# Delta-rule triangular solve: full 128 by 128 tiles against packed 64 by 64 blocks

## The reference, cut to what matters

```python
decay = jnp.exp(jnp.where(incl, gcum[..., :, None] - gcum[..., None, :], -jnp.inf))
kb = kc * bc[..., None]
a_mat = jnp.where(strict, jnp.einsum('nbhid,nbhjd->nbhij', kb, kc) * decay, 0.0) \
    + jnp.eye(c, dtype=jnp.float32)
rhs = jnp.concatenate([vc * bc[..., None], kb * jnp.exp(gcum)[..., None]], axis=-1)
sol = lax.linalg.triangular_solve(a_mat, rhs, left_side=True, lower=True, unit_diagonal=True)
u_val, k_cum = sol[..., :dv], sol[..., dv:]
qk = jnp.where(incl, jnp.einsum('nbhid,nbhjd->nbhij', qc, kc) * decay, 0.0)
```

## Time and profile before

| quantity | value |
|---|---|
| median of 3 runs | 1184.05 us (1181.15 to 1190.07) |
| the profiled execution, its own time | 1182.57 us |
| its span in the trace | 1180.8 us |
| PE busy | 1133.2 us (96%) |
| PE weight loads busy | 1029.1 us (87%) |
| DVE busy | 768.0 us (65%) |
| ACT busy | 553.0 us (47%) |
| the chain that ended last | PE 80%, DVE 12%, ACT 4%, issue 3%, DMA 1% |

### The profile page before, as it was taken

The page is one execution under the profiler, slowest core; times in us unless marked ns, Lnnn a source line. Parts: engine busy times, 40 slices in busy tenths (PEclk is TensorE's granted clock), DMA queues, the critical chain, the costliest instruction groups (busy, mean ns, idle before and its releaser), DMA issues.

```text
span 1180.8 us, 17834 instructions
## 1 busy us (share of the span) xinstructions
PE 1133.2 (96%) x7630; PEld 1029.1 (87%) x7630; DVE 768.0 (65%) x914; ACT 553.0 (47%) x639; POOL 45.2 (4%) x108
## 2 busy tenths in 40 slices
PE   7989998999999999999998899999999999999996
PEld 6888887898899899998788789999888998999995
DVE  4585767664477898887577565455556866555544
ACT  5466554332444444434564454444445565444443
POOL 8000000000000000000002200000000000000000
PEclk9999999999999999999999999999999999999999
DMA  7765864265354555555453355556543435566551
GB/s 248 201 165 78 130 142 115 56 124 87 112 193 154 188 185 196 183 179 178 147 189 123 127 180 179 182 194 193 179 143 107 142 110 178 181 192 195 182 178 54
DMA packets 128448, 185.08 MB, mean 157 GB/s; under 512 B 6868, under 2 KB 104161, under 8 KB 128370
## 3 DMA queue, kind: packets, MB, share of 16 engines
q1 hardware_dynamic: 123136, 182.46, 52.1%
q10 hardware_dynamic: 4690, 1.36, 0.5%
q0 software_dynamic: 544, 0.13, 0.1%
HBM read 182.89 MB, written 1.05 MB: 156 GB/s over the span
## 4 chain that ended last, share of the span: by engine, by line
PE 80%; DVE 12%; ACT 4%; issue 3%; DMA 1%; ACTq 0%; SPq 0%; DVEq 0%
PE ps L1916 13%; PE ps L1917 13%; PE ps L1918 13%; PE ps L1933 10%; PE ps L1934 10%; PE ps L1935 10%; DVE low L1278 4%; ACT whi L902 1%; PE ps L2250 1%; PE ps L1949 1%; PE ps L2120 1%; PE ps L2126 1%; PE ps L2129 1%; DMA raw<-in_w_in 1%; PE ps L1902 1%
## 5 line engine op out<-in xcount | busy, mean ns | idle before, releaser
L902 ACT ACTIVATE whi<-raw 128x2048 fp32r<-128x2048 f32 x172 | 328.0, 1912 | 346.2 <-PE ps L1918 169.8
L1278 DVE TENSOR_TENSOR low<-raw,whi 128x2048 fp32r<-128x2048 f32 x172 | 394.2, 2295 | 51.8 <-ACT whi L902 48.8
L1916 PE MATMUL ps<-hhi,whi 128*128 128x256 f32 x1424 | 410.3, 288 | 5.1 <-DVE low L1278 3.2
L1917 PE MATMUL ps<-hlo,whi 128*128 128x256 f32 x1424 | 405.7, 285 | 0.0
L1918 PE MATMUL ps<-hhi,low 128*128 128x256 f32 x1424 | 405.5, 285 | 0.0
L1916 PEld LDWEIGHTS ps<-hhi,whi 128*128 128x128 f32 x1424 | 275.6, 194 | 11.4 <-issue 4.7
L1917 PEld LDWEIGHTS ps<-hlo,whi 128*128 128x128 f32 x1424 | 275.8, 194 | 1.7 <-issue 0.2
L1918 PEld LDWEIGHTS ps<-hhi,low 128*128 128x128 f32 x1424 | 275.7, 194 | 0.0
L1933 PE MATMUL ps<-whi,ahi 128*128 128x512 f32 x416 | 163.9, 394 | 5.6 <-issue 1.8
L1934 PE MATMUL ps<-low,ahi 128*128 128x512 f32 x416 | 162.4, 390 | 0.0
L1935 PE MATMUL ps<-whi,alo 128*128 128x512 f32 x416 | 162.0, 390 | 0.0
(11 more groups left out here) (381 smaller groups left out, 1189.9 us busy)
## 6 DMA issues: line engine op xcount, KB each, us to landing
raw<-in_ffn_w SPq DMA_DIRECT2D x64, 1024.0 KB, 5.3
raw<-in_w_in SPq DMA_DIRECT2D x32, 1024.0 KB, 10.4
raw<-in_w_up SPq DMA_DIRECT2D x22, 1024.0 KB, 4.9
raw<-in_gla_w_in SPq DMA_DIRECT2D x12, 1024.0 KB, 5.2
raw<-in_w_down SPq DMA_DIRECT2D x11, 1024.0 KB, 4.8
raw<-in_ab_w_in SPq DMA_DIRECT2D x8, 1024.0 KB, 5.2
raw<-in_w_branch SPq DMA_DIRECT2D x6, 1024.0 KB, 5.8
raw<-in_w_o SPq DMA_DIRECT2D x4, 1024.0 KB, 4.8
```

The source lines that it names most:

```text
L902: act.activation(whi[:, u % SPLIT, :], raw[:, u % RAW, :], ACT.Copy).then_inc(sem("hi_done"), 1)
L1278: dve.tensor_tensor(wlo[:, u % RAW, :], raw[:, u % RAW, :], whi[:, u % SPLIT, :].bitcast(F32), ALU.subtract).then_inc(sem("lo_done"), 1)
L1916: pe.matmul(out, wh, hi[:, k0 + k, :], start=k == 0, stop=False)
L1917: pe.matmul(out, wh, lo[:, k0 + k, :], start=False, stop=False)
```

## The change

The chunk matrices are kept packed: partitions 0 to 63 hold the 64 by 64 matrices of the tile's first chunk, partitions 64 to 127 those of the second, heads side by side, so an array is 128 partitions by 256 columns. `chunks` are the two slices of 64 partitions. A product over four heads is issued as eight source matmuls (two chunks per head), each with rows 0 to 63 and columns 0 to 63 of the array, or rows 64 to 127 and columns 64 to 127, in turn. GpSimd makes packed copies of three constants, and `dn_pre(0)` on DVE waits for them. The key-key products use all 128 rows and one half of the columns; the second product of `dn_sol` uses one half of the rows and all columns and writes two banks. The order of the two z products and of the two updates is exchanged, and the last level leaves out X. `dn_x0` becomes a matmul with the packed identity in place of a transpose. The table of steps is the same.

```diff
+        def packed(one, half):
+            return by(one[:, half * DH * CH:(half + 1) * DH * CH], DH)
...
+        levp = own_[3][:, 0:6 * CH].rearrange("p (l j) -> p l j", l=6)
+        trip, idp = own_[3][:, 6 * CH:7 * CH], own_[3][:, 7 * CH:8 * CH]
+        chunks = [slice(CH * b, CH * b + CH) for b in range(P // CH)]
...
+            for c_ in chunks:
+                then(pool.tensor_copy(trip[c_, :], tri[c_, c_]))
+                then(pool.tensor_copy(idp[c_, :], ident[c_, c_]))
+                then(pool.tensor_copy(levp[c_, :, :], lev[c_, :, c_]))
...
             def dn_y(t, l):
                 act.wait_ge(sem("dn_BX"), 2 * (l - 1) + t + 1)
-                act.activation(Y[t], by(ps[:, 7 - t, :], DH), ACT.Copy).then_inc(sem("dn_Y"), 1)
+                act.activation(Y[t], packed(ps[:, 7 - t, :], 0), ACT.Copy).then_inc(sem("dn_Y"), 1)
...
             def dn_decay(t):
                 dve.wait_ge(sem("dn_eg"), t + 1)
-                link(dve.tensor_tensor(DT[t], by(ps[:, grow_bank[t], :], DH),
-                                       wide(gcol[:, t, :].unsqueeze(2), [DH, P]), ALU.subtract))
+                for c_ in chunks:
+                    ins = dve.tensor_tensor(DT[t][c_], by(ps[c_, grow_bank[t], :], DH)[:, :, c_],
+                                            gcol[c_, t, :].unsqueeze(2).to_broadcast([CH, DH, CH]), ALU.subtract)
+                link(ins)
...
             def dn_z(t, l):
                 n_ = 2 * (l - 1) + t + 1
-                dve.wait_ge(sem("dn_XBX"), 2 * n_)
-                own(dve.tensor_tensor(XT[t], XT[t], by(ps[:, 2 * t, :], DH), ALU.subtract), "dn_X2", 2 * n_ - 1)
-                own(dve.tensor_tensor(X[t], X[t], by(ps[:, 2 * t + 1, :], DH), ALU.subtract), "dn_X2", 2 * n_)
+                last = l == LEVELS - 1
+                if not last:
+                    dve.wait_ge(sem("dn_XBX"), 2 * n_ - 1)
+                    own(dve.tensor_tensor(X[t], X[t], packed(ps[:, 2 * t + 1, :], 0), ALU.subtract), "dn_X2", 2 * n_ - 1)
+                done = 4 * (l - 1) + t + 1 if last else 2 * n_
+                dve.wait_ge(sem("dn_XBX"), done)
+                own(dve.tensor_tensor(XT[t], XT[t], packed(ps[:, 2 * t, :], 0), ALU.subtract), "dn_X2", done)
...
             def dn_decay(t):
                 pe.wait_ge(sem("dn_gb"), 2 * t + 2)
-                pe.matmul(by(ps[:, beta_bank[t], :], DH), ones[:, :], XT[t], start=True, stop=True)
+                for c_ in chunks:
+                    pe.matmul(packed(ps[c_, beta_bank[t], :], 0), ones[c_, 0:CH], XT[t][c_], start=True, stop=True)
...
             def dn_kk(t):
                 for j in range(2):
                     for h in range(DH):
+                        for c_ in chunks:
+                            cols_ = slice(t * P + c_.start, t * P + c_.stop)
+                            ins = pe.matmul(ps[c_, kk_banks[t][j], h * CH:(h + 1) * CH], dnT[:, DH + h, cols_],
+                                            dnT[:, (DH if j == 0 else 0) + h, cols_], start=True, stop=True)
...
             def dn_z(t, l):
+                if l < LEVELS - 1:
+                    for h in range(DH):
+                        for c_ in chunks:
+                            ins = pe.matmul(ps[c_, 2 * t + 1, h * CH:(h + 1) * CH], XT[t][c_, h, :], Y[t][c_, h, :],
+                                            start=True, stop=True)
+                    ins.then_inc(sem("dn_XBX"), 1)
+                for h in range(DH):
+                    for c_ in chunks:
+                        ins = pe.matmul(ps[c_, 2 * t, h * CH:(h + 1) * CH], Y[t][c_, h, :], XT[t][c_, h, :],
+                                        start=True, stop=True)
                 ins.then_inc(sem("dn_XBX"), 1)
...
             def dn_sol(t):
-                pe.wait_ge(sem("dn_X2"), 2 * (8 + t + 1))
+                pe.wait_ge(sem("dn_X2"), 4 * (LEVELS - 2) + t + 1)
                 if t:
-                    pe.wait_ge(sem("dn_u"), t)
                     pe.wait_ge(sem("dn_kcT"), t)
                 for h in range(DH):
-                    ins = pe.matmul(ps[:, 6, h * P:(h + 1) * P], XT[t][:, h, :], vb[:, t, h, :], start=True, stop=True)
+                    for c_ in chunks:
+                        ins = pe.matmul(ps[c_, 2 * t + 1, h * P:(h + 1) * P], XT[t][c_, h, :], vb[c_, t, h, :],
+                                        start=True, stop=True)
                 for h in range(DH):
-                    ins = pe.matmul(ps[:, 7, h * P:(h + 1) * P], rhsk[:, t, h, :], XT[t][:, h, :], start=True, stop=True)
+                    for b, c_ in enumerate(chunks):
+                        ins = pe.matmul(ps[:, 6 + b, h * CH:(h + 1) * CH], rhsk[c_, t, h, :], XT[t][c_, h, :],
+                                        start=True, stop=True)
```

More of the change, by code:

```diff
@@ L16 @@
 SPLIT = 3
+LEVELS = 6
 LEAD = 2
@@ L662, in build @@
         flat = [cy[:, i, :, :].rearrange("p a t -> p (a t)") for i in range(2)]
-        DT = [by(one, DH) for one in (flat[1], own_[3])]
-        X, XT, LT, Bl, Y = [[by(one, DH), by(two, DH)] for one, two in
-                            zip(own_[0:3] + flat, tops + [own_[3]])]
+        def packed(one, half):
+            return by(one[:, half * DH * CH:(half + 1) * DH * CH], DH)
+        X, XT, LT, Bl = [[packed(a_, k), packed(b_, k)] for a_, b_, k in
+                         ((own_[0], tops[0], 0), (own_[1], tops[1], 0), (own_[1], tops[1], 1), (flat[0], tops[2], 0))]
+        Y = DT = [packed(flat[1], 0), packed(tops[2], 1)]
+        grows = [by(own_[0], DH), by(tops[0], DH)]
+        dnout = by(own_[2], DH)
+        levp = own_[3][:, 0:6 * CH].rearrange("p (l j) -> p l j", l=6)
+        trip, idp = own_[3][:, 6 * CH:7 * CH], own_[3][:, 7 * CH:8 * CH]
+        chunks = [slice(CH * b, CH * b + CH) for b in range(P // CH)]
         S = by(xs[:, 1, 0:512], DH)
@@ L1580, in dn_y @@
             def dn_y(t, l):
[L1581 removed]
+                dve.tensor_tensor(Bl[t], LT[t], wide(levp[:, l, :].unsqueeze(1), [DH, CH]), ALU.mult)\
                    .then_inc(sem("dn_B"), 1)
@@ L1629, in dn_out @@
                     dve.wait_ge(sem("dn_hi"), t)
-                own(dve.scalar_tensor_tensor(out=XT[0], in0=by(ps[:, 6, :], DH), scalar=col("dn_gain", 0),
+                own(dve.scalar_tensor_tensor(out=dnout, in0=by(ps[:, 6, :], DH), scalar=col("dn_gain", 0),
                                              in1=zT[:, :, t * P:(t + 1) * P], op0=ALU.mult, op1=ALU.mult),
@@ L2089, in dn_decay @@
                     pe.wait_ge(sem("dn_tok"), 6)
-                pe.matmul(by(ps[:, beta_bank[t], :], DH), ones[:, :], XT[t], start=True, stop=True)
-                pe.matmul(by(ps[:, grow_bank[t], :], DH), ones[:, :], X[t], start=True, stop=True)\
+                for c_ in chunks:
+                    pe.matmul(packed(ps[c_, beta_bank[t], :], 0), ones[c_, 0:CH], XT[t][c_], start=True, stop=True)
+                pe.matmul(by(ps[:, grow_bank[t], :], DH), ones[:, :], grows[t], start=True, stop=True)\
                   .then_inc(sem("dn_grow"), 1)
@@ L2125, in dn_z @@
                 for h in range(DH):
-                    ins = pe.matmul(ps[:, 2 * t, h * P:(h + 1) * P], Y[t][:, h, :], XT[t][:, h, :], start=True, stop=True)
-                ins.then_inc(sem("dn_XBX"), 1)
-                for h in range(DH):
-                    ins = pe.matmul(ps[:, 2 * t + 1, h * P:(h + 1) * P], XT[t][:, h, :], Y[t][:, h, :], start=True, stop=True)
+                    for c_ in chunks:
+                        ins = pe.matmul(ps[c_, 2 * t, h * CH:(h + 1) * CH], Y[t][c_, h, :], XT[t][c_, h, :],
+                                        start=True, stop=True)
@@ L2164, in dn_state @@
                         pe.matmul(out, dnT[:, h, c * CH:(c + 1) * CH], S[:, h, :], start=True, stop=False)
-                    ins = pe.matmul(out, qkT[own_, t, h, own_], vb[own_, t, h, :], start=c == 0, stop=True)
+                    ins = pe.matmul(out, qkT[own_, t, h, 0:CH], vb[own_, t, h, :], start=c == 0, stop=True)
                 ins.then_inc(sem("dn_o"), 1)
```

54 lines of the change are left out of this document (30 added, 24 removed).

## The result

Changed kernel: 1173.66 us median (1172.41 to 1175.25, 4 runs) against 1184.05 (1181.15 to 1190.07, 4 runs, one more than in the table ahead of the prediction); ratio 0.9914, 95% interval 0.9889 to 0.9939. The predicted 1167 was 6.7 too low. The range of 1163 to 1181 held the time, its likeliest part of 1163 to 1171 did not. The gain is 10.4 us, 0.86%; I had given 0.69 to a gain of over 1%. Run again beside another set of runs of before it came to 0.9904 (0.9874 to 0.9934), 11.7 us.

A forecast was written before the change was run, and what follows sets the result against it. PE, busy 96% of the span, was taken as the bound, with DVE ahead of level 1. Gains summed to 16.8 us: 1165.8 on the profiled execution, 1167 as median; range 1163 to 1181, likeliest 1163 to 1171.

The forecast's parts named there:

- The pair of quarters: PE's solve products: two opposite quarter instructions run side by side at 0.060 us a pair, a product 0.48 instead of 0.89.
- (b): Levels 1 and 2 of the solve: level 1 4.3 us instead of 7.98, level 2 3.2 instead of 5.44; gain 5.9.
- (c): Later levels, 3 to 5: cheaper and fewer products, each block paying 0.2 us for array changes; gain 7.2 us.
- Quarters take turns: Rival for PE's solve products: quarters writing one PSUM bank exclude each other, a product stays 0.9 us; time 1182; chance 0.13.
- Weight loads don't shrink: Rival for PE's solve products: a pair costs 0.109 us, products stay 0.87, gain 5.8, time 1178; chance 0.10.
- slower: Rival for all solve products on PE: turns at 0.112 us an instruction, a product 1.8; 24 us slower, 1208; chance 0.07.
- DVE and ACT: Operations of the solve: DVE at 256 columns 0.42 us instead of 0.69, ACT's copy out of PSUM 0.37 instead of 0.60.
- (a): Stretch up to level 1: DVE would allow a start 4.2 us earlier, PE ends just behind DVE; gain 3.7 us.
- (d): Last step of the solve: eight pairs 0.87 us as now, the wait of 0.78 for ACT stays; gain 0.
- The granted clock falls: Case for the solve: little-streaming quarter products bring one or two clock falls, 1.7 us each; 1169 to 1170; chance 0.15.
- Transfers: Weight transfers over the solve move forward with PE: DMA share about 0.55, ACT's splits never waiting for a transfer.

The follow-up runs named there:

- experiment 2: Changed kernel with every solve product issuing all heads of one chunk, then all of the other, instead of alternating quarters: 1184.99 us, ratio 0.9999 to the kernel before.
- experiment 4: Changed kernel with the first kk multiplication on DVE done twice per tile, two more operations ahead of level 1: 1174.33 us in one run.
- experiment 7: Changed kernel, last step's tiles half a unit apart, next level's B computed before the updates: 1173.56 us with levels 1 and 2 on end, 1170.28 with them apart.
- experiment 8: Kernel before with output-step transposes repeated, 304 or 112 more matmuls after 300 us: first small step at 62.73 or 61.24 us, against 59.5 before.
- experiment 1: Both kernels run again unaltered: changed 1172.74 us, before 1186.54 us (ratio 1.0016 to before).

## Why the prediction was right, and where it missed

**The pair of quarters** (0.060, from bounds of 0.055 and 0.109) measured 0.058, the product 0.47 (0.48). Forecast right, and with it the whole of (b) and (c) as far as PE's work goes: 3.6 for 3.7, 1.9 for 1.9, 2.4 for 2.4, 3.1 for 2.9. (By its own prices (c) adds up to 7.5 and not 7.2; 7.4 were measured.) The LDWEIGHTS rule of the Trainium skill (TensorE: Matmul & The Clock Gate), load time by the columns of the weights, agrees with the measured pair.

**Quarters take turns** (0.13) is refuted: pairs that write one PSUM bank on different partitions start 6 to 23 ns apart and go at 0.058 a pair, the pitch at which one quarter alone goes in experiment 2. By the rule of the Trainium skill (TensorEngine Tiling, Restrictions and Gotchas) on row tiles and one bank they could not; the measurement decides. My reading, that the rule is about outputs that meet, fits and was not tested. **Weight loads don't shrink** (0.10) and **slower** (0.07, from 135 ns a pair) fall with the same number.

**DVE and ACT** took 0.42 and 0.385 for 0.42 and 0.37. **(a)** gave 3.2 for 3.7: DVE gave 3.8 by the start of B (B of level 1 issued 18.29 after the transposes, 22.09 before) where I had 4.2, and my walk of PE had PE just behind DVE. That was the wrong way round: PE waits 0.5, 0.9 and 0.8 for DVE there, and experiment 4 shows that DVE's time comes through whole.

**(b), the step that failed:** level 2 with its unit gave 0.8 for 2.2. The two levels themselves are as forecast (4.33 for 4.3; 3.18 for 3.2). What failed is the sentence that the instruction count costs nothing, its cover being that instructions to different parts start almost together. That said how PE executes them, not how it gets them. 300 more matmuls and as many loads cost twice, the first by the reading in experiment 7 and the second by experiment 8: 1.4 us in the stall behind level 2, where PE had been through 200 matmuls and as many loads in 7.4 us (second table, `x198` and `x192`), and 2 to 3 us at the start of the kernel, for the length of the program. Together about 4 of the 6.7 us by which the prediction was low. (a) and (d) are 0.7 more. Some 2 us are left, which no experiment pins down; the lower mean clock of experiment 1 is the candidate.

**(d)** 0 for -0.2: right. **The granted clock falls** (0.15, one or two falls, 1169 to 1170): not in the solve, where the clock is 1.00 in both traces of the changed kernel, but at the start, at 15 us, for 3.4 us, which I had not thought of. PE had just waited 2.75 us there for its first unit. The wait alone does not explain the fall: with 112 more matmuls PE waited 2.72 at the same place, and the clock stayed up. The trace of before with its falls was one draw of several; the profiled execution of after had 17.1 us of falls before the solve instead of 10.2.

**Transfers:** the share in the rest of the solve is 0.54 (0.55 forecast), and no split waits for a transfer.

**The sum** for the median: 14.8 of the region, less 2.4 for the start-up, leaves 12.4; measured 11.7 in the repeated pair and 10.4 in the first. What is left, 0.7 to 2, is the size of one fall of the clock, for instance the one near 640 us that both traces of the changed kernel have and the first of before has not. That it is this fall is not shown: the second trace of before has one near 658.

**The range.** It reached up to 1181 for quarters that take turns and weight loads that do not shrink. Neither came true, and it was two costs that no rival named which took the time out of the likeliest part. The mechanism of the solve was foreseen (14.8 us of 16.8); that the time still lay in the range is partly luck.

## What to carry to other kernels

Block-diagonal products are worth packing on opposite quarters if the quarters alternate instruction by instruction: two blocks at once, half the columns, 0.47 for 0.89 us. Count instructions as a cost of their own: in a dense stretch of short ones PE can stand as if it had outrun their fetch, and then a wait closed inside the stretch is lost again at its end (1.2 won, 1.4 more of stall in experiment 7). Half a unit of long instructions between dense stretches cut the stall from 1.44 to 1.60 us down to 0.66 to 0.87, for one more change of array shape. Before taking a wait's whole length as a gain, look for the next one: the wait for B moved on by a level when the levels were put apart, and went only when B was computed ahead of the updates.

## What the runs showed of the hardware that was not expected

- Grouped by quarter, the same product takes 0.575 us instead of 0.47: some three instructions of the next quarter run beside the last three of this one, not all eight.
- In this stretch a fetch of 16 KB of instructions took 0.9 to 1.0 us, and PE went on 1.2 to 1.5 us after its last packet, behind the same matmul in seven traces. There is one fetch for about 250 matmuls and loads.
- A program longer by 304 matmuls and loads that run after 300 us slows the transfers of the first 14 us from 267 to 207 GB/s and delays PE by 2.4 to 3.3 us at 60 us; 112 more cost 0.9 to 1.8.
- The same code had from 10.2 to 20.4 us at half clock between 60 and 190 us in the four traces of the two kernels; each fall costs about half its length.
